# Prompt attention heads paired across the two partition halves, their score products in separate PSUM banks

## What is computed

```python
s = einsum('bnqkgd,bnskd->bnkgqs', qb, kk) * SCALE + bias   # qb: 128 queries, kk: 128 or 256 keys, d = 64
p, lse = softmax_stats(s, mask, sink)
o = einsum('bnkgqs,bnskd->bnqkgd', p, vv)
```

## Time and profile before

| | |
|---|---|
| median of three runs | 1713.55 us |
| profiled execution, its own time | 1710.16 us |
| its span | 1708.1 us |
| prompt attention loop (first L1712 to last L1658) | 275.8 to 418.2 us |
| routed experts | about 920 to 1670 us |

### The profile page before, as it was taken

How to read it: one execution, slowest core, us unless ns; L and a number is a source line. 1 busy time by engine, 2 the same in 40 slices (tenths; PEclk the granted TensorE clock), 3 DMA queues, 4 the chain that set the end, 5 groups by cost and what they waited for, 6 DMA issues and landing times.

```text
span 1708.1 us, 21951 instructions
## 1 busy us (share of the span) xinstructions
PE 1597.3 (94%) x6939; PEld 974.9 (57%) x6940; DVE 536.1 (31%) x988; ACT 301.5 (18%) x751; POOL 523.7 (31%) x676
## 2 busy tenths in 40 slices
PE   4899999998799999999997999999999999999990
PEld 3577888876677777764553444444444444444440
DVE  3212002276320211125883222232222233332324
ACT  4100002265230000012410111111111111111111
POOL 2240000032000000000104555555555555555540
PEclk8899999999899999999998999999999999999995
DMA  9667967151989943143205989999899989999935
GB/s 314 219 226 273 316 220 247 40 187 62 260 274 291 326 140 95 44 142 122 93 1 211 381 297 339 353 342 311 275 338 311 331 289 338 337 336 331 343 114 190
DMA packets 153463, 412.48 MB, mean 241 GB/s; under 512 B 24283, under 2 KB 90183, under 8 KB 127633
## 3 DMA queue, kind: packets, MB, share of 16 engines
q1 hardware_dynamic: 126635, 326.40, 52.8%
q0 software_dynamic: 26768, 85.25, 17.5%
HBM read 397.59 MB, written 99.27 MB: 291 GB/s over the span
## 4 chain that ended last, share of the span: by engine, by line
PE 83%; DMA 9%; SPq 4%; DVE 2%; issue 1%; POOL 0%; ACT 0%; POOLq 0%; DVEq 0%; ACTq 0%
PE bank L2066 80%; DMA arena<-in_we_down 5%; SPq L732 1%; DMA arena<-in_cache_b 1%; SPq L714 1%; PE bank L2260 1%; PE bank L2319 1%; PE bank L2640 1%; DMA arena<-in_state_pool 1%; DMA arena<-in_w_ada 1%; DMA yacc<-arena,scol 0%; DVE arena L2056 0%; DMA arena<-yacc 0%; SPq L719 0%; SPq L771 0%
## 5 line engine op out<-in xcount | busy, mean ns | idle before, releaser
L2066 PE MATMUL bank<-arena 128*128 128x288 f32 (+12 forms) x6252 | 1522.9, 427 | 33.9 <-DMA arena<-in_w_ada 9.6
L2066 PEld LDWEIGHTS bank<-arena 128*128 128x128 f32 (+5 forms) x6252 | 890.3, 175 | 602.2 <-issue 487.7
L1155 POOL DMA_INDIRECT arena<-h2rows,icol x288 | 292.9, 1017 | 128.7 <-issue 68.7
L1180 POOL DMA_INDIRECT yacc<-arena,scol x70 | 112.1, 1601 | 205.8 <-DVE arena L2020 183.4
L1085 POOL DMA_DIRECT2D out<-in_cache_b x24 | 11.9, 500 | 449.0 <-PE bank L2066 448.7
L2009 DVE STREAM_TRANSPOSE arena<-arena 128x1024 f32<-128x1024 f32 x70 | 141.7, 2024 | 19.5 <-DMA arena<-h2rows,icol 19.5
L2014 DVE TENSOR_TENSOR arena<-bank,arena 128x256 f32<-128x256 f32 x70 | 29.7, 424 | 333.4 <-ACT arena L1477 333.4
L1221 ACT ACTIVATE arena<-bank 128x512 f32<-128x512 f32 (+6 forms) x147 | 72.7, 501 | 327.4 <-PE bank L2066 215.7
L2020 DVE TENSOR_SCALAR arena<-bank,arena 128x512 f32<-128x512 f32 x70 | 52.5, 751 | 191.0 <-PE bank L2066 191.0
L1477 ACT ACTIVATE arena<-bank 128x256 f32<-128x256 f32 x70 | 26.8, 383 | 443.9 <-PE bank L2066 443.9
L1533 DVE COPY arena<-bank 128x512 f32<-128x512 f32 (+7 forms) x60 | 35.0, 586 | 195.5 <-PE bank L2066 128.4
(11 more groups left out here) (251 smaller groups left out, 595.0 us busy)
## 6 DMA issues: line engine op xcount, KB each, us to landing
arena<-in_we_gate SPq DMA_DIRECT2D x64, 1024.0 KB, 7.2
arena<-in_we_up SPq DMA_DIRECT2D x64, 1024.0 KB, 10.3
arena<-in_we_down SPq DMA_DIRECT2D x64, 1024.0 KB, 15.6
out<-in_cache_b POOLq DMA_DIRECT2D x8, 4080.0 KB, 15.7
arena<-in_w_ada SPq DMA_DIRECT2D x12, 2048.0 KB, 10.5
arena<-in_cache_b SPq DMA_DIRECT2D x96, 256.0 KB, 5.0
arena<-in_w_in SPq DMA_DIRECT2D x7, 2048.0 KB, 21.7
arena<-in_w_in SPq DMA_DIRECT2D x24, 512.0 KB, 6.9
```

The costliest lines, as they stand in the source:

```text
L1155: pool.indirect_dma_start(xg[:, j, 256 * g:256 * g + 256], None, quarters, bass.IndirectOffsetOnAxis(ap=icol[:, 4 * j + g:4 * j + g + 1], ...
L1180: pool.indirect_dma_start(yacc[j], bass.IndirectOffsetOnAxis(ap=scol[:, j:j + 1], axis=0), yb[:, j, :], None, bounds_check=TOK - 1, oob_is ...
L2066: return pe.matmul(out, lhsT, rhs, start=first, stop=last)
```

## The change

Pairs are now 2p and 2p + 1 in B, p and p + 4 in C, so that the two heads of a pair lie in opposite halves of the partitions, and so in the upper and the lower 64 rows of the array. Each score product has a bank of its own: S(s) fills banks 0 and 1 in even steps, 2 and 3 in odd ones, and VectorE reads both in one instruction. The ring is given up inside the loop: T(s-2) goes to bank 4 + s % 2, O(s-3) to bank 6 + s % 2, and whatever comes beside or after a unit to bank 4 + (s + 1) % 2. O streams the 64 columns of the head alone. Bias tables, sinks, and the places of the outputs follow the new pairs; the number and size of the transfers stay.

```diff
         if s < len(UNITS):
-            fill(("S", s), "D")
+            fill(("S", s), "D", 2 * (s % 2))
         if 0 <= s - LAGT < len(UNITS):
-            fill(("T", s - LAGT), "A")
+            fill(("T", s - LAGT), "A", 4 + s % 2)
         if 0 <= s - LAGO < len(UNITS):
-            fill(("O", s - LAGO), "D")
+            fill(("O", s - LAGO), "D", 6 + s % 2)
         for key in after_unit(s - LAGO):
-            fill(key, "A")
+            fill(key, "A", 4 + (s + 1) % 2)
         for key, who in beside_unit(s):
-            fill(key, who)
+            fill(key, who, 4 + (s + 1) % 2)
...
 def heads(unit):
     kind, _, p = unit
-    return [2 * p, 2 * p + 1] if kind == "C" else [p, p + 2]
+    return [p, p + 4] if kind == "C" else [2 * p, 2 * p + 1]
...
-                if PLAN[m][2] == bank:
+                if PLAN[m][2] == bank or PLAN[m][0][0] == "S" and PLAN[m][2] + 1 == bank:
                     wait_emptied(pe, PLAN[m][0])
...
-                own = 64 * (p // 2) if kind == "C" else 64 * p
-                own = bank[:, 0:2 * P].rearrange("p (h d) -> p h d", h=2)[:, :, own:own + HD]
+                own = bank[:, 0:2 * HD].rearrange("p (h d) -> p h d", h=2)
...
-                    bank = wait_fill(dve, ("S", s))
+                    wait_fill(dve, ("S", s))
+                    pair = banks[:, 1024 * (s % 2):1024 * (s % 2) + 1024].rearrange("p (h c) -> p h c", h=2)[:, :, lo:w]
...
-                    dve.scalar_tensor_tensor(view(to), view(bank[:, 0:2 * w]), SCALE, view(bias),
+                    dve.scalar_tensor_tensor(view(to), pair, SCALE, view(bias),
                                              ALU.mult, ALU.add).then_inc(emptied["D"], 1)
...
-                    bank = bank_for(pe, ("S", s))
+                    bank_for(pe, ("S", s))
+                    if s < 2:
+                        for m in PLAN[:INDEX[("S", s)]][::-1]:
+                            if m[2] == 2 * s + 1:
+                                wait_emptied(pe, m[0])
+                                break
...
-                        ins = mm(bank[:, h * w + lo:h * w + lo + width], q, kT[rows, ck, k0:k0 + width], True, True)
+                        ins = mm(psb[2 * (s % 2) + h][:, lo:lo + width], q, kT[rows, ck, k0:k0 + width], True, True)
...
-                        col = 768 if kind == "C" else 256 * kind + P * (hd // 2)
+                        col = 768 + HD * (hd // 4) if kind == "C" else 256 * kind + HD * hd
                         for i, (kt, _) in enumerate(blocks):
-                            ins = mm(bank[:, P * h:P * h + P], pTb[:, u % 2, n * P:(n + 1) * P],
-                                     vTM[:, kt, col:col + P], i == 0, i == len(blocks) - 1)
+                            ins = mm(bank[:, HD * h:HD * h + HD], pTb[:, u % 2, n * P:(n + 1) * P],
+                                     vTM[:, kt, col:col + HD], i == 0, i == len(blocks) - 1)
```

More of the change, by code:

```diff
@@ L398, in build @@
         pairs = sb("pairs", [P, 2], I32)
-        psb = [ctx.enter_context(nc.psum_tensor(f"bank{n}", [P, 512], F32))[:, :] for n in range(8)]
+        banks = ctx.enter_context(nc.psum_tensor("bank", [P, 8 * 512], F32))
+        psb = [banks[:, 512 * n:512 * n + 512] for n in range(8)]
         bmask_b = misc[:, 0:8]
@@ L790, in spread_bias @@
                         if n < 2:
-                            h, off, w, pos = n + 2 * j, 127, 256, 256 * j
+                            h, off, w, pos = 2 * n + j, 127, 256, 256 * j
                         elif n < 4:
-                            h, off, w, pos = 4 * (n - 1) + j // 2 + 2 * (j % 2), 255, 128, 128 * j
+                            h, off, w, pos = 4 * (n - 1) + j, 255, 128, 128 * j
                         else:
-                            h, off, w, pos = 12 + 2 * (n - 4) + j, 127, 256, 256 * j
+                            h, off, w, pos = 12 + (n - 4) + 4 * j, 127, 256, 256 * j
                         sp.dma_start(biasP[:, n, pos:pos + w],
@@ L1312, in _ @@
                         for h in range(2):
-                            act.activation(dsk[:, s % 4, h:h + 1], sinkb[:, 2 * p + h:2 * p + h + 1], ACT.Exp,
+                            act.activation(dsk[:, s % 4, h:h + 1], sinkb[:, p + 4 * h:p + 4 * h + 1], ACT.Exp,
                                            scale=-1.0, bias=nmx[:, s % 4, h:h + 1])
@@ L1657, in outputs @@
                     link(dve.reciprocal(rden[:, u % 4, 0:2], rden[:, u % 4, 0:2]))
-                    dve.tensor_tensor(octok[:, t % 2, 128 * p:128 * p + 128].rearrange("p (h d) -> p h d", h=2),
+                    dve.tensor_tensor(octok[:, t % 2, :].rearrange("p (h q d) -> p h q d", h=2, q=4)[:, :, p, :],
                                       own,
@@ L1663, in outputs @@
                     to = stage[:, kind, t * 264:(t + 1) * 264]
-                    dve.tensor_copy(to[:, 256 + p:260:2], nmx[:, u % 4, 0:2])
-                    dve.tensor_copy(to[:, 260 + p:264:2], den[:, u % 4, 0:2])
-                    dve.tensor_copy(to[:, 0:256].rearrange("p (h g d) -> p h g d", h=2, g=2)[:, :, p, :],
+                    dve.tensor_copy(to[:, 256 + 2 * p:258 + 2 * p], nmx[:, u % 4, 0:2])
+                    dve.tensor_copy(to[:, 260 + 2 * p:262 + 2 * p], den[:, u % 4, 0:2])
+                    dve.tensor_copy(to[:, 128 * p:128 * p + 128].rearrange("p (h d) -> p h d", h=2),
                                     own).then_inc(emptied["D"], 1)
@@ L1718, in _ @@
                         link(ins)
-                        ins = dve.tensor_tensor(nm, nm, sinkb[:, 2 * p:2 * p + 2], ALU.min)
+                        ins = dve.tensor_tensor(nm, nm, sinkb[:, p:8:4], ALU.min)
                     ins.then_inc(max_ready, 1)
```

## The result

The changed kernel takes 1741.31 us (median of four executions, of which three lie between 1740.48 and 1742.11). An execution more than 1.5% above the fastest of its kernel stands in no comparison; here that is the fourth, with 3363.29 us. The kernel before took 1715.91 beside it. The ratio is 1.0133, with a 95% interval of 1.0095 to 1.0172: **slower by 1.3%**, where 1710.3 us and no measurable change were forecast.

The account below looks back on a forecast made before the run. TensorE was taken to bound the loop up to step 28, VectorE largely after; 0.9 + 1.6 - 1.9 + 4.3 - 2.0 + 0.4 = 3.3 us gained, from 1713.55 to 1710.3 us, range 1705.5 to 1719.5.

Parts of the forecast that it names:

- Score products: Attention loop: two of S's four instructions hidden, saving 0.43 us wide, 0.21 narrow, 0.46 strided; at most 16.4 us.
- a rival from it, that only half the saving comes: Score products overlap only in part, half the saving: sum -0.7 us, time 1714.3 us; chance 0.20.
- Output products: O with 64 columns: no gain taken, as the weight load sets the pace, 0.105 us per instruction.
- O shrinks too: Each O instruction saves about 0.055 us where TensorE binds, some 7 us more: 1703 us; chance 0.07.
- (a): Fills beside steps 0 to 12: 0.9 us gained in 0 and 1, none in 2 to 8, 1.6 after.
- (b): Step 14: kT and kTs share a bank, so kTs waits for ScalarE; loss 1.9 us, S(13) to S(15) savings included.
- (e): Step 37: four bT fills share one bank, each waiting for ScalarE's copy; loss 1.9 to 2.2, taken as 2.0 us.
- the stall's effect on the clock: Clock falling to 1.2 GHz at the wait in (e) would cost 0 to 2 us, taken as 0.
- (c): Steps 16 to 28 run on TensorE: a step falls from 2.54 to 2.11 us, 4.3 us gained.
- (d): Steps 29 to 34: VectorE sets the pace, so nothing is gained.
- (f): S(39), heading a chain through VectorE and ScalarE to the loop's end: 0.4 us gained.
- The sum: All loop terms together with full overlap: 3.3 us gained, 1710.3 us on the median; chance 0.60.

Follow-up runs that it names:

- fastest run: Changed kernel with O of 128 columns, kT, kTs and bT banks mended, kTs in step 20, 18 useless transposes ahead of three ocT: 1707.15 us, ratio 0.9929.
- last run: The fastest run's kernel, but with output products of 64 columns: 1717.45 us, ratio 0.9978 to the kernel before.

## Why the prediction was wrong

It was wrong by 31 us and in its sign of change; of its terms most were right where a run shows them at full clock.

**Score products: right, to 0.01 us.** Full overlap was taken, with S at 0.63 wide. The fastest run shows 0.64 wide and 0.43 narrow. The Trainium skill says ("TensorE: Matmul & The Clock Gate", Part 3: Packing small matmuls) that matmuls start and end strictly in program order; the prediction drew a rival from it, that only half the saving comes. The pieces above speak against that rival: the saving is the full one, for strided weights too (a step beside a kvc fill is 4.57 + 0.37 us after and 5.03 + 0.37 before, 0.46 less). In the changed kernel itself the full saving shows only ahead of 351 us.

**Output products: right in the instructions, wrong in the worth.** 0.105 us per instruction were read from the router's products, and 0.105 was measured. "I take no gain" held; that half the columns at the same pace could be a loss was not asked. The rival "O shrinks too" is out.

**(a) Steps 0 to 12: right.** The transposes of step 13 start at 347.66 us before and at 344.46 after, 71.9 and 68.5 us behind the loop's first scale-and-bias: 3.4 gained, against 2.5 from (a) and 0.5 from S(13). TensorE did wait for q's copies, as said: 2.1 us in seven waits in the loop.

**(b) kTs: right in what waits for what and in its price as a wait, low in the idle time, and cut off too early.** From T at step 13 (3.4 us ahead) to T(13) at 351.23 (1.2 us ahead of its 352.23, both from the loop's first instruction) the loss is 2.2 us. The 1.9 of the prediction takes in what S(13) saves, 0.46, which is behind us there; counted like it, the loss is 1.7. The prediction had held GpSimd's zeros in place; they hang on a TensorE product and came 2.75 us sooner, but TensorE stood for 2.71 us and not for 1.5 to 2. **The step that failed** is the next one: this wait was priced at its length, and its effect on the clock was considered only for (e), as "0 to 2 us, taken as 0". What came in its place is 92.2 us at half clock, and a loop that grew by 25.6 us. The argument had been that TensorE idled twice for about 1.8 us and kept 1.00; that was true of a loop whose output products stream 128 columns. The kernel before with 64 columns, and the same idle places, lost the clock at 385.5 us. And with the old pairs and 128 columns, the new wait alone put the clock at half for 23.9 us. So the two terms that were each taken as nothing, the narrow O and the stall's effect on the clock, make the loss together: give O its 128 columns back, and the whole change is at 0.9991.

**(c) Steps 16 to 28: right in the pieces, never seen in the changed kernel.** In the fastest run, at full clock, the step is 0.59 + 1.53 = 2.12, as predicted (2.11); in the changed kernel it was 3.79.

**(d) Steps 29 to 34: not as said in the changed kernel.** VectorE was to set the pace. At half clock TensorE did: busy 29.06 of 30.8 us from 389.2 to 420.0, where it had been busy 15.48 of 19.10 in the VectorE-bound stretch.

**(e) Four bT in one bank: right.** From the end of S(37) to the start of S(38) 5.65 us were worked out; in the changed kernel it was 6.56, from 423.88 to 430.44, but at half clock. The run with O of 128 columns has the same banks and passes this place at a granted clock of 1.00. Its chain gives 410.34 - (403.09 + 1.55) = 5.70:

```profile
403.09 1.55 PE bank L2070 x12
...
410.34 0.63 PE bank L2070 x4
```

**(f)** lies at half clock in the changed kernel, and no run prices it by itself.

**The sum.** 3.3 us gained is the forecast for a clock that holds, and no run shows the changed kernel at one. The loop lost 25.6 instead, so by this estimate the clock took some 29 us. In the fastest run, with O of 128 columns, the banks mended and idle time filled, the loop came to 130.0 us, 5.8 less than before; there the losses of (b) and (e) are gone too.

That TensorE's share of the span on the profile's page (94% and 93%) shows none of this is worth noting: at half clock the engine looks just as busy. The Trainium skill has a case that is near ("TensorE: Matmul & The Clock Gate", A second HAM failure mode: psum-queue depth-cycling): TensorE that idles briefly again and again because it cycles through PSUM banks lets its clock swing. The trace agrees in part: a wait for a PSUM bank, 2.71 us ahead of kTs, came before the fall. What came behind it is another thing than a swing, and the measurement decides: the clock stayed at half for 92.2 us, with TensorE busy for 37.97 of the first 38.1.

**Open.** Why the narrow output products keep the clock down: the runs show that they do, not by what, and the pairs have a part in it too. The clock came back with narrow O after 13.6 us in one run, and in the changed kernel when the score products had ended. Where the slower executions of the last run lose the clock. Whether the bT bank alone, without kTs, would lose it. Whether fewer columns in other products than O do the same; that was not tried.

## What to carry to other kernels

Price a new wait on a busy TensorE not by its length alone: read the granted clock behind it, stretch by stretch, and ask what work follows, since here that decided how soon the clock came back. Cutting streamed columns that cost no time (here 128 to 64, at 0.105 and 0.111 us per instruction) saved nothing and kept the clock down longer. Where a short wait can't be avoided, a few transposes into a bank that will be overwritten held the clock at 1.00 over it, at no cost that shows.

## What was not expected of the hardware

TensorE busy for 37.97 of 38.1 us at half clock, with output products of 64 columns, did not bring the clock back. Behind a wait at the same place, with 128 columns, it was back after 6.8 us in one run and 23.9 us in another. A wait of 1.7 us in the kernel before cost about 15 us in the median. And 18 to 24 transposes without use were enough to hold the clock over a wait.
